# A decoder layer's down projection as seven half-size products, their operand sums made by GpSimd and by accumulating DMAs

## The reference, cut to what matters

```python
D_MODEL = 1024
D_FF = 2816
def conv_ffn(hn, w_up, conv_w, conv_b, w_down):
    u = causal_dwconv(hn @ w_up.astype(hn.dtype), conv_w) + conv_b.astype(hn.dtype)
    a, b = jnp.split(u, 2, axis=-1)
    return (jax.nn.silu(a) * b) @ w_down.astype(hn.dtype)
...
h = h + conv_ffn(rmsnorm(h, norm2[layer]), w_ffn_up[layer], ffn_conv_w[layer], ffn_conv_b[layer], w_ffn_down[layer])
h = rmsnorm(h, norm_f)
return h[:, N_META:]
```

## Time and profile before

| what | us |
|---|---|
| median of 3 runs | 2037.92 (2035.79 to 2041.82) |
| the profiled execution's own time | 2038.91 |
| its span, first to last instruction | 2037.1 |
| last up matmuls / first down matmul | 1772.3 |
| TensorE busy in the span | 1983.4 (97%) |
| VectorE, ScalarE, GpSimd busy | 1220.9, 770.8, 287.2 |

### The profile page before, as it was taken

One profiled execution on the slowest core, in us unless ns is written; L12 is line 12 of the kernel. 1 busy time (PEld: TensorE's weight loads), 2 busy tenths in 40 slices (PEclk: granted clock), 3 DMA queues, 4 the chain that ended last, 5 costly groups with the idle time before them and its releaser, 6 DMA issues.

```text
span 2037.1 us, 31749 instructions
## 1 busy us (share of the span) xinstructions
PE 1983.4 (97%) x13268; PEld 1902.2 (93%) x13268; DVE 1220.9 (60%) x1476; ACT 770.8 (38%) x1022; POOL 287.2 (14%) x276
## 2 busy tenths in 40 slices
PE   8999999999999999999999999997999999999998
PEld 8999998999999999899999999997999999988886
DVE  6457674666577555666533343389888787743533
ACT  5213333534333444434343333244444444332322
POOL 0000003659280122222000001100000000000101
PEclk9999999999999999999999999998999999999999
DMA  9235567664456664555342223311222221274442
GB/s 285 87 108 130 147 164 194 194 197 156 149 148 161 159 180 148 149 156 169 92 183 99 83 91 88 100 60 56 84 73 84 73 90 67 85 282 139 142 144 108
DMA packets 271619, 270.21 MB, mean 133 GB/s; under 512 B 147772, under 2 KB 215716, under 8 KB 271348
## 3 DMA queue, kind: packets, MB, share of 16 engines
q1 hardware_dynamic: 271476, 268.17, 43.0%
HBM read 188.55 MB, written 79.57 MB: 132 GB/s over the span
## 4 chain that ended last, share of the span: by engine, by line
PE 87%; DVE 6%; issue 2%; DMA 2%; ACT 2%; SPq 2%; DVEq 0%; ACTq 0%
PE a_psum L1046 32%; PE a_psum L1349 18%; PE a_psum L1358 12%; PE a_psum L154 10%; PE a_psum L1033 5%; PE a_psum L1121 1%; PE a_psum L1140 1%; PE a_psum L1225 1%; PE a_psum L1150 1%; PE a_psum L1103 1%; PE a_psum L1118 1%; PE a_psum L1166 1%; DMA w_raw<-in_w_in 1%; DVE ext L2097 1%; PE a_psum L1240 1%
## 5 line engine op out<-in xcount | busy, mean ns | idle before, releaser
L1046 PE MATMUL a_psum<-xh,w_hi 128*128 128x342 f32 (+3 forms) x1656 | 536.2, 324 | 1.4 <-DVE w_lo L1789 1.3
L1046 PE MATMUL a_psum<-xl,w_hi 128*128 128x342 f32 (+3 forms) x1656 | 531.9, 321 | 0.0
L1046 PE MATMUL a_psum<-xh,w_lo 128*128 128x342 f32 (+3 forms) x1656 | 530.0, 320 | 0.0
L1046 PEld LDWEIGHTS a_psum<-xh,w_hi 128*128 128x128 f32 x1656 | 312.7, 189 | 4.2 <-DVE w_lo L1789 1.9
L1046 PEld LDWEIGHTS a_psum<-xl,w_hi 128*128 128x128 f32 x1656 | 312.8, 189 | 1.0
L1046 PEld LDWEIGHTS a_psum<-xh,w_lo 128*128 128x128 f32 x1656 | 312.6, 189 | 0.0
L1493 ACT ACTIVATE post<-a_psum 128x342 f32<-128x342 f32 (+3 forms) x207 | 94.4, 456 | 553.3 <-PE a_psum L1046 516.5
L1789 DVE TENSOR_TENSOR w_lo<-w_raw,w_hi 128x1024 fp32r<-128x1024 f32 x87 | 110.2, 1267 | 153.6 <-ACT w_hi L1418 153.6
L1358 PE MATMUL a_psum<-act_hi,down_hi 128*128 128x512 f32 x352 | 139.7, 397 | 3.4 <-DVE act_lo L2298 3.4
L1358 PE MATMUL a_psum<-act_hi,down_lo 128*128 128x512 f32 x352 | 139.7, 397 | 0.0
L1358 PE MATMUL a_psum<-act_lo,down_hi 128*128 128x512 f32 x352 | 139.2, 396 | 0.0
(11 more groups left out here) (272 smaller groups left out, 3921.2 us busy)
## 6 DMA issues: line engine op xcount, KB each, us to landing
w_raw<-in_w_in SPq DMA_DIRECT2D x76, 512.0 KB, 3.8
down_raw<-in_w_ffn_down SPq DMA_DIRECT2D x44, 512.0 KB, 3.6
up_raw<-in_w_up SPq DMA_DIRECT2D x19, 1024.0 KB, 4.9
mix_scratch<-post SPq DMA_DIRECT2D x32, 522.0 KB, 2.8
act_scratch<-post SPq DMA_DIRECT2D x22, 512.0 KB, 2.6
act_raw<-act_scratch SPq DMA_DIRECT2D x44, 256.0 KB, 3.9
ext<-mix_scratch SPq DMA_DIRECT2D x9, 1024.0 KB, 7.0
y<-mix_scratch SPq DMA_DIRECT2D x18, 512.0 KB, 5.8
```

Source lines behind the costliest of these rows:

```text
L1046: mm = pe.matmul(psum[:, u % 2, 0:n], w[:, k, :], x[:, k, at0:at0 + n], start=(k == 0 and part == 0), stop=(k == KC - 1 and part == 2))
```

## The change

The output, act and w_down are cut into quadrants, and the eight quadrant products become seven (KH = 11 row blocks each, so NDOWN = 77 steps), each step half as large: 128 x 512 of weights, 128 x 512 of activations, 4 output blocks x 3 matmuls of 512 columns. Four products take operands that are sums of quadrants.

- **Weight sums.** GpSimd issues, during the projections of the first stage, four DMAs that copy quadrants of w_down (1408 x 512) to an HBM scratch ws, and then, later in the kernel, four DMAs that add quadrants to those copies (`accum_op=ALU.add`).
- **Activation sums.** After each `gate_product(j)` GpSimd makes one difference of 128 x 512 (j < 11) or three (j >= 11), SP stores each to an HBM scratch ts and, for j >= 11, loads two operands back first. ScalarE's `first_tap(j, 1)` waits, for j > 11, until the sums of j - 1 are stored.
- **Start of the down stage.** Three steps (DEARLY) are prepared on ScalarE and VectorE where one was, `down_low(3)` stands between the two taps of the last block, `load_down(0)` to `load_down(3)` stand ahead of the last store, and the table load moves ahead of `down_high(3)`.
- **Residual.** It is loaded in 8 DMAs of 512 KB between the steps' loads, where one of 4096 KB was.
- **Combining.** One Copy of 4 banks on ScalarE and eight operations of 4 banks on VectorE (`down_add`), at fixed steps; three squares of 4 banks.
- **Last product in column halves.** In the last four steps the 4 banks are done for 256 columns first and then for the other 256, so adds, squares, sums, roots and finishes of the end are of 256 columns.
- Semaphores p_q2 and p_qd become one, p_q.

```diff
-NDOWN = 2 * FT
-DW, DA, DIN = 6, 8, 3
+KH = FT // 2
+NDOWN = 7 * KH
+DW, DA, DIN, DEARLY = 8, 8, 3, 3
...
+            def load_sums(j):
+                k = j - KH
+                sp.wait_ge(act_st[k % 2], 16 * (k // 2 + 1))
+                sp.wait_ge(sum_st, sums_stored(j - 1))
+                sp.dma_start(ts_one[:, :], sc["act"][k][:, 512:1024]).then_inc(sum_in, 16)
+                sp.dma_start(ts_two[:, :], sc["ts"][0, k]).then_inc(sum_in, 16)
+
+            def store_sums(j):
+                for n, (kind, x) in enumerate(((0, ts_one),) if j < KH else
+                                              ((2, ts_one), (1, ts_two), (3, acc_of(j, 1)[:, 0:512]))):
+                    sp.wait_ge(p_q, summed_act(j) if j < KH else summed_act(j - 1) + n + 1)
+                    sp.dma_start(sc["ts"][kind, j % KH], x[:, 0:512]).then_inc(sum_st, 16)
...
             for i in range(NPAIR):
+                j = J0 + i
                 if 2 <= i + 1 < NPAIR:
                     load_pair(i + 1)
-                store_act(J0 + i - 1)
+                store_act(j - 1)
+                store_sums(j - 1)
+                if j >= KH:
+                    load_sums(j)
...
-            load_down(0)
-            load_down(1)
+            for q in range(DEARLY + 1):
+                load_down(q)
             store_act(FT - 1)
-            for q in range(2, NDOWN):
+            store_sums(FT - 1)
+            for q in range(DEARLY + 1, NDOWN):
                 load_down(q)
-                if q == 5:
-                    sp.dma_start(res[:, :, 2 * H2 - SEQ:2 * H2], sc["hres"].rearrange("m p t -> p m t")).then_inc(h_in, 16)
+                if q % 3 == 1 and q < 3 * KC + 4:
+                    m = (q // 3 + 3) % KC
+                    sp.dma_start(res[:, m, 2 * H2 - SEQ:2 * H2], sc["hres"][m]).then_inc(h_in, 16)
...
+            def right_sums():
+                pe.wait_ge(o_sum, 9)
+                pe.matmul(roots_at(0), ones, sq22[:, 0, :], start=True, stop=False)
+                pe.matmul(roots_at(0), ones, sq12[:, 0, :], start=False, stop=True).then_inc(o_ss, 1)
...
-            for m in range(KC):
-                for q in range(NDOWN - TAIL, NDOWN):
-                    down_block(q, m, False)
-                if m == 2:
-                    sums(0)
-            sums(1)
+            for ch in range(2):
+                for m in range(4):
+                    if ch:
+                        pe.wait_ge(added, C12_DONE + m + 1)
+                    for q in range(NDOWN - TAIL, NDOWN):
+                        mm = down_step(q, m, 256 * ch, 256)
+                    mm.then_inc(d_bank, 1)
+                    if ch == 1 and m == 1:
+                        left_sums(0)
+            left_sums(1)
...
-                    down_high(0)
+                    for q in range(DEARLY):
+                        down_high(q)
                 first_tap(j, 0)
 
             first_tap(FT - 1, 1)
             gate_silu(FT - 1)
-            for q in range(1, FT + 6):
+            table(LNEXP)
...
-                    down_low(0)
+                    for q in range(DEARLY):
+                        down_low(q)
                 combine(i, 3)
...
             combine(NPAIR - 1, 4)
             taps(FT - 1, 0)
+            down_low(DEARLY)
             taps(FT - 1, 1)
             gate_product(FT - 1)
...
+            for j in range(FT):
+                a0, left, right = acc_of(j, 0), slice(0, 512), slice(512, 1024)
+                pool.wait_ge(prod, j + 1)
+                if j < KH:
+                    if j:
+                        pool.wait_ge(sum_st, sums_stored(j - 1))
+                    pool.tensor_tensor(ts_one[:, :], a0[:, left], a0[:, right], ALU.subtract).then_inc(p_q, 1)
+                else:
+                    pool.wait_ge(sum_in, 16 * (NCH + 2 * (j - KH + 1)))
+                    pool.tensor_tensor(ts_one[:, :], a0[:, right], ts_one[:, :], ALU.subtract).then_inc(p_q, 1)
+                    pool.tensor_tensor(ts_two[:, :], ts_two[:, :], a0[:, right], ALU.add).then_inc(p_q, 1)
+                    pool.wait_ge(p_q, summed_act(j - 1) + 2)
+                    pool.tensor_tensor(acc_of(j, 1)[:, left], ts_two[:, :], a0[:, left], ALU.subtract).then_inc(p_q, 1)
```

More of the change, by code:

```diff
@@ L981, in load_down @@
             def load_down(q):
-                half, kb = q // FT, q % FT
+                p, k = q // KH, q % KH
+                if q == KH:
+                    sp.wait_ge(w_sums, 128)
                 if q >= DIN:
                     sp.wait_ge(da_hi, q - DIN + 1)
[L985 to L994, removed]
@@ L1352, in _, with down_step @@
                     mm.then_inc(pe_p, 1)
-            def down_block(q, m, last):
-                half, kb = q // FT, q % FT
+            def down_step(q, m, c0=0, n=512):
+                p, k = q // KH, q % KH
                 w, x = q % DW, q % DA
-                for part, (a, b) in enumerate(((dw_high[w], da_high[x]), (dw_high[w], da_low[x]), (dw_low[w], da_high[x]))):
-                    mm = pe.matmul(psum[:, m, :], a[:, m * P:m * P + P], b[:, :], start=(kb == 0 and part == 0),
-                                   stop=(kb == FT - 1 and part == 2))
-                if kb == FT - 1:
-                    mm.then_inc(d_bank, 1)
-                elif last:
-                    mm.then_inc(d_used, 1)
@@ L1365, in sums @@
-            def sums(half):
-                pe.wait_ge(added, KC + 1 + half)
-                pe.wait_ge(o_sum, 5 * half + 5)
-                pe.matmul(psum[:, half, :], ones, o_sum2[half], start=True, stop=False)
-                for n in range(2):
-                    pe.wait_ge(o_sqd, 8 * half + 7 + n)
-                    mm = pe.matmul(psum[:, half, :], ones, o_sq67[half][n], start=False, stop=(n == 1))
+                hi, lo = (y[w][:, m * P:m * P + P] for y in (dw_high, dw_low))
+                for part, (a, b) in enumerate(((hi, da_high[x]), (hi, da_low[x]), (lo, da_high[x]))):
+                    mm = pe.matmul(psum[:, (0, 4, 0, 4, 0, 4, 0)[p] + m, c0:c0 + n], a, b[:, c0:c0 + n],
+                                   start=(p not in (2, 5, 6) and k == 0 and part == 0),
+                                   stop=(k == KH - 1 and part == 2), skip_group_check=(p in (2, 5, 6)))
@@ L1764, in roots @@
-            def roots(half):
-                act.wait_ge(o_ss, half + 1)
-                root = psum[:, half, :]
-                act.activation(root, root, ACT.Ln, bias=eps, scale=1.0 / D).then_inc(o_rms, 1)
-                act.wait_ge(o_rms, 2 * half + 1)
-                act.activation(root, root, ACT.Exp, scale=-0.5).then_inc(o_rms, 1)
-            for m in range(KC):
-                square(m, 0)
-                down_high(FT + 6 + m)
-            for q in range(FT + 6 + KC, NDOWN):
-                down_high(q)
@@ new lines, in _ @@
+            for q in range(DEARLY, NDOWN):
+                if q == KH + 4:
+                    act.wait_ge(d_bank, 1)
+                    act.activation(d_one[:, :, :], psum[:, 0:4, :], ACT.Copy).then_inc(c11, 1)
+                down_high(q)
+                if q == 3 * KH + 5:
+                    square(0)
+                if q == 5 * KH + 5:
+                    square(1)
+                if q == 6 * KH + 4:
+                    square(2)
+            roots(0)
+            for ch in range(2):
+                for m in range(4):
+                    act.wait_ge(added, C12_DONE + 4 * ch + m + 1)
+                    act.activation(sq21[:, m, 256 * ch:256 * ch + 256], out_cols(4 + m, 1 + ch), ACT.Square).then_inc(o_sqd, 1)
+                    if ch == 1 and m == 2:
+                        roots(1)
@@ L1782, in _ @@
+            roots(2)
         @block.vector
@@ L2361, in _ @@
+            for m in range(4, KC):
+                finish(1, m)
+            for m in range(KC):
+                finish(2, m)
         @block.gpsimd
```

272 lines of the change are left out of this document (173 added, 99 removed).

## The result

The changed kernel takes 2043.98 us in the median of 11 runs. The kernel before, run 11 times beside it, takes 2038.63, and the ratio of the two is 1.0024 (95% interval 1.0017 to 1.0032). The forecast was 2019.3, range 2007 to 2030. What the change does to TensorE came as forecast; a term that was set at 0 cost 22 us.

The account below looks back on a forecast made before the run. TensorE was taken as the bound, with 87% of the span. Terms -30.1 + 0.4 + 13.3 - 3.4 + 1.2 = -18.6 us took the profiled 2038.9 to 2020.3, or 2019.3 against the median; range 2007 to 2030.

Parts of the forecast that it names:

- The accumulating DMAs: GpSimd's weight-sum DMAs during the projections: taken to cost 0, bounds 0 and 8 us.
- waits for w_lo in the front: Sign of a wrong prediction: TensorE waiting in the front for low parts of weight tiles.
- the start of the down stage: Queue-by-queue walk after block 20's product: losses of 19.3 us against 6.0 before, so +13.3 us; bounds 0 and +22.
- the DMAs of GpSimd disturb the front: Rival, front: TensorE waits for weights while they run; 2049 if ten tiles are 3 us late each; chance 0.05.
- TensorE's work: Down stage: 876 matmuls of 512 columns and 96 of 256 replace 1056: -30.1 us; sums over partitions +0.4.
- the walk: Start of the down stage, queue by queue: TensorE waits 2.0, 2.9 and 9.4 us, plus 2.5 twice at lower clock.
- The tail: Last down matmul to the end: 12.0 us becomes 8.6 with 256 columns, -3.4; sixteen other finishes beside the last four steps.
- GpSimd's sums: Up stage: hidden in VectorE's slack except in the first pairs, where two sums cost +1.2 us (0 to 2).
- the bound of the up stage: Rival: for j >= 11 GpSimd's sums limit the pairs if each takes over 4.0 us; 2052 at 5; chance 0.08.
- The steady part: Down steps after the start: loads and splits keep ahead of TensorE's 2.77 us a step; taken as 0, upper bound 1.5.
- The wait of `first_tap` for stored sums: Up stage: sums landed at 1767.3, the tap comes at 1772.5, so 5 us cover the wait.
- The starved case: Rival: long landings at the start (+9), feed bound (+1.5), pairs (+1), DMAs (+8), more than half together: 2024 to 2034; chance 0.15.

Follow-up runs that it names:

- e1: Changed kernel with GpSimd's four weight copies and first two accumulating DMAs moved out of the front to late tiles: 2022.27 us, 0.9925 of before.
- e2: Changed kernel with only the first two accumulating DMAs moved late, the four copies left at tile 5: 2023.24 us, 0.9930 of before.
- e4: Changed kernel with SP's loads of down steps 4 to 6 issued ahead of block 21's stores: 2033.47 us, 0.9980 of before.
- e5: e1 and e4 together, plus loads of down steps 0 to 2 ahead of block 20's stores: 2007.01 us, 0.9852 of before.
- e6: e5 with the second roots one square earlier and VectorE's second finishes spread around the last add: 2006.03 us, 0.9844 of before.
- e8: e1 without GpSimd's sums of blocks 1 and 2, their stores and waits kept (wrong values): 2020.30 us, 0.9917 of before.
- e11: Changed kernel with the rk tile's turned stores in packets of 512 bytes, not 128 (elements out of place): 2036.63 us, 0.9996 of before.
- e10: Changed kernel with the two accumulating DMAs at tile 12 in packets of 512 bytes, not 2 KB: 2040.16 us, 1.0009 of before.
- e7: Changed kernel with the first two accumulating DMAs at tile 8 in place of tile 12: 2033.93 us, 0.9980 of before.
- e3: Changed kernel with the two accumulating DMAs at tile 12 made plain copies (weight sums lack terms): 2029.81 us, 0.9959 of before.

## Why the prediction was wrong

**The step that failed** is "The accumulating DMAs": "I take 0; bounds 0 and 8 us (8 weight tiles late by 1 us each)". It was 21.7 us, over the upper bound, and e1 takes it away whole. The prediction's own sign of being wrong, waits for w_lo in the front, is the first row of the waits. Two things were wrong in it. It asked whether weights would land late, and they did (the copies), for 0.3 us (e2). It did not go through SP's list to ask which instruction is held when the DMA engines are shared, as the same text did for the start of the down stage. What is held is a run of stores in packets of 128 bytes, and behind it, in one queue, the next weights. And the row it leaned on, TensorE full at 25 to 50 us beside DMA engines at 0.97, had the warning beside it, in SP's timeline of the kernel before, which the prediction does not use:

```profile
9.40 23.55 SPq L752 DMA_DIRECT2D vt_scratch<-ext  x1
```

There one issue took SP 23.55 us. It stands behind a store of 2592 KB, and from 8 to 34 us SP's queue moved 5837 packets of under 512 bytes. So a run of small packets held SP in the kernel before too, with no other queue beside it; TensorE was busy for 23.89 of the 24 us from 9 to 33, so it cost nearly nothing there. The rival "the DMAs of GpSimd disturb the front" had the outcome (2049 against 2044) at a chance of 0.05, by another way: ten tiles late by 3 us each, where it was one tile late by 25.

**TensorE's work and the start of the down stage** were right: -17.3 against -16.4. The waits of the walk came within 1 us each. Part of the agreement is two errors that offset each other: the three waits are 1.5 us longer than forecast, and the matmuls behind them 0.2292 us apart and not 0.2312, 1.6 us in 780. e4 and e5 show the cause of the waits, SP's order, since moving the loads alone takes 8.3 us of the span and the full reorder 16.2 us (spans of e1 and e5, 14.3 apart, and 1.9 of different fronts) with one wait of 3.1 left.

**The tail** was mis-sized: -1.4 against -3.4. The term put the sixteen other finishes beside the last four steps; only the eight of the first sum were there, and the eight of the second ran behind the last matmul. e6 gets 1.5 of it back.

**GpSimd's sums** at the first pairs: 2.05 us where the term had 1.2 (0 to 2), by the mechanism that it named (e8). As the bound of the up stage they were far off: 1.6 to 1.75 us a sum against the 4.0 from which it decides.

**The steady part** was fed, as forecast: no wait stands in its 792 matmuls, and they are 0.2292 us apart at full clock against 0.2312 before. The wait of `first_tap` for stored sums ends nothing on the chain.

**One number of the prediction does not follow from its terms.** The starved case adds up to 19.5 us (9 + 1.5 + 1 + 8); more than half of it would be 2029 to 2039, not 2024 to 2034.

What stays open: that DMA engines take turns between queues by the packet fits the counts (1469 to 1467, 952 to 946, 1583 to 1586) and e11, and the time of e10 only in part. What in SP's queue makes an issue wait, and how full it must be, no row shows. Why the matmuls stand closer than before, no run shows.

The version of e6 beats both kernels: 0.9844 of before, 32 us. Against the changed kernel it is 38.0 us, and 38.4 in the spans, which the profiles divide into 21.5 for when the weight sums run, 15.4 for the order of the loads and 1.5 for the tail.

## What to carry to other kernels

Here a background DMA could not be priced by the bytes it moves or by the share of the DMA engines; what counted was whose packets it met. So look in the issuing queues for runs of small-packet transfers and for what stands in order behind them. The same DMAs cost 21.7 us at one place and 1.6 at another. Every transfer put into a kernel's slack needs the walk through the queues at the place where it runs, as much as the place that it is meant for.

## What the runs showed of the hardware that was not expected

- One issue of the sync engine, of a 2 KB store behind one of 128 KB in 128-byte packets, took up to 10.98 us (e7) while 2 KB packets of another queue were on the DMA engines, against 0.56 us without them.
- With packets waiting in both queues the profile counts them one for one, whatever their sizes: 1469 of 2 KB to 1467 of mostly 128 bytes in 15 us (changed kernel), 1583 of 512 bytes to 1586 in 5 us (e10).
- 11.5 MB of plain DRAM copies, with the DMA engines at a share of 1.02, cost the front 0.3 us (e2), though three weight loads landed in 9.6 to 10.0 us, where the median of all is 3.9.
- Accumulating DMAs of 2816 KB, DRAM to DRAM, land 19.5 to 25.2 us after their issue; issued right behind another of the kind, 38.4 to 42.5 us. Plain copies at the same place (e3) take 17.3 and 23.8 us.
- One GpSimd sum of 512 elements took from 1.26 us (VectorE idle) to 3.30 us, and an addition of VectorE beside it 1.79 in place of 0.68.
